# Relative bias of the neighbourhood heads: added by VectorE to mirrored scores instead of by flip products on TensorE

## The chip, the cores and the metric

One core of one Trainium2 chip runs the whole program. The metric is the device time of one launch in microseconds, median over runs. The kernel before takes 879.6 us (three runs, 878.18 to 881.19).

## The reference

Two layers (DEPTH = 2) of a pre-norm encoder on one sequence of 256 tokens (a grid of 4 rows by 64 columns), width 1024, all float32:

```python
for l in range(DEPTH):
    h = rms_norm(x, norm1_g[l])
    aq, ak, av, bq, bk, bv, cq, ck, cv, c_q, c_kv, k_rope = split(h @ w_in[l])
    o_a = global attention (RMS-normed, axially rotated q and k), 4 heads
    o_b = neighbourhood_attention(bq, bk, bv, b_rel_bias[l]), 4 heads
    o_c = windowed attention with a distance penalty and a sink, 4 heads
    o_d = latent attention (low-rank q and kv, shared rotary key), 4 heads
    y = einsum(stack(o_a, o_b, o_c, o_d), w_branch[l])
    g = sigmoid(h @ w_gate[l] + b_gate[l])
    x = x + sum_n(g * y) @ w_o[l]
    h2 = rms_norm(x, norm2_g[l])
    x = x + square(relu(h2 @ w_ff1[l])) @ w_ff2[l]
return rms_norm(x, final_g)
```

In the neighbourhood attention a query at grid row r and column c sees all 4 rows (the window of 8 is cut to the grid's 4) and 16 columns clamped to the grid. To the scaled score with the key at row kr, column kc it adds `rel_bias[head, kr - r + 7, kc - c + 15]`, from a table of 15 x 31 for each head. Every other key is out.

## The kernel before

**Numbers.** Each float32 product with weights is made of three products of a high and a low part (`split_product`, L1035 to L1037). ScalarE rounds a chunk of weights to its high part (`split_hi`, w_hi, L537), VectorE subtracts for the low part (`split_lo`, w_lo, L734). The weights come in chunks of 1 MB (w_in: 1.05 MB, 8 chunks of 268 columns), each in two halves, by SP's queue into `raw`, which holds two chunks. A half is loaded again as soon as VectorE has made the low part of what it held. w_hi and w_lo are rings of four chunks, so TensorE can be up to three chunks behind the splits.

**Stages.** The mixer part of a layer is a list of steps that all engines walk in program order: steps 0 to 7 are the eight chunks of w_in (`project`, tokens on the partitions: first half for token tile 0, second for tile 1; ScalarE copies the first out at L671, VectorE the second at L959), then 16 gate chunks and the four branch products `y`. In a step each engine also does a piece of the attention. The heads go in pairs: the pair j has its scores on TensorE (`scores`) in step 8 + 2j, its softmax on VectorE and ScalarE (`maxima`, `exps`, `normalise`) a step later, its transposes of the probabilities (`turn_prob`) in step 10 + 2j, its values a step after that. Pairs 0 and 1 are of mixer A, 2 and 3 of B (the neighbourhood heads, n = 1), 4 and 5 of C, 6 and 7 of D. Small transposes and products (`small`) go through one bank, bank_x; ScalarE empties it (`evac`), and the next of them waits for that. On ScalarE the order in step 6 is: `evac` of aq (the transposed queries of mixer A), copy of the projection's first half, `split_hi` of chunk 9. In step 5 it is: copy, `split_hi` of chunk 8, the first gate chunk.

**The bias.** POOL issues 16 DMAs in each layer (L493, after `rs_a`, that is in step 3), one for each head, token tile and grid row of queries, each from 64 overlapping runs of the table into 64 partitions: 4 key rows of 64 elements (256 bytes) for each partition. The partition axis counts the queries backwards, so that the address in the table rises with the partition. When all 16 are in, POOL adds the column mask `window` (L498). TensorE then starts the scores of the B pairs with a product of `flip` (the reversed identity times 8, the inverse of the scale) with the bias (L1118), which turns the rows round and adds them, and accumulates the scores on top (L1126). A score product runs on two 64-row halves of TensorE, a flip product on all 128 rows. The buffer `bias` is used again for `qd` and `kd`, the latent mixer's queries and keys, which ScalarE writes from step 15 on (uq0, L584).

**What sets the order.** The order on each engine is the order of the code. VectorE and ScalarE wait for semaphores only, and an instruction that waits holds up all behind it on its engine. POOL's `norm` and `inverse_root` (L453) make the reciprocal roots that the norms need.

Of the kernel before, what the change touches and what calls it, by code (L numbers as in the profile page):

```python
# [34 lines left out]
BIAS_ROW = 2 * NA_COLS - 1  # L35
WINDOW = 128
# [91 lines left out]
C_FLIP = C_WIN + GRID_W  # L128
C_N = C_FLIP + P

# [5 lines left out]
DVE_LINKS, POOL_LINKS = 50, 12  # L136


def constants():
# [19 lines left out]
    def tiles(a):  # L159
        return a.reshape(T, P, -1).transpose(1, 0, 2).reshape(P, -1)  # L160

    parts = [np.eye(P, dtype=np.float32), tiles(np.concatenate([rc, cc], 1)), tiles(np.concatenate([rs, cs], 1)),
             tiles(dc), tiles(ds), tiles(dist), window, np.eye(P, dtype=np.float32)[::-1] * HD ** 0.5]
# [5 lines left out]
def trunk_kernel(nc, x, norm1_g, w_in, w_gate, b_gate, a_q_norm_g, a_k_norm_g, b_rel_bias, c_sink,  # L169
# [3 lines left out]
    with ctx:  # L173
# [21 lines left out]
        bias = sb("bias", [P, H, T * SEQ])  # L195
        bias_flat = bias[:, :, :].rearrange("p a b -> p (a b)")
# [12 lines left out]
        tmp = sb("tmp", [P, 2, 512])  # L209
        vd = sb("vd", [P, T, H, HD])  # L210
# [36 lines left out]
        flip = cst[:, C_FLIP:C_FLIP + P]  # L247
# [72 lines left out]
        stored = sem("stored")  # L320

        def f32(ap):
            return ap.bitcast(F32)
# [100 lines left out]
        def _(pool):  # L424
# [40 lines left out]
            with pool.Fori(0, DEPTH) as l:  # L465
                norm(2 * l, l)

                pool.dma_start(gain_qk[:, 0, :], a_q_norm_g[bass.ds(l, 1), :].to_broadcast([P, HD])).then_inc(gains_landed, 16)
# [13 lines left out]

                for hd in range(H):
                    for t in range(T):
                        for r in range(2):
                            row = 2 * t + 1 - r
                            at = (NA_ROWS - 1 - row) * BIAS_ROW + NA_COLS - 1 - (GRID_W - 1)
                            table_h = b_rel_bias[bass.ds(l, 1), hd]
                            src = bass.AP(tensor=table_h.tensor, offset=table_h.offset + at,
                                          ap=[[1, GRID_W], [BIAS_ROW, ROWS], [1, GRID_W]])  # L490
                            dst = bias[r * GRID_W:(r + 1) * GRID_W, hd, t * SEQ:(t + 1) * SEQ].rearrange(
                                "p (r c) -> p r c", c=GRID_W)
# [12 lines left out]
                for k in range(4 * (NB - 1)):  # L505
                    pool.wait_ge(y_read, l * 16 + (k + 5))
                    if k >= 4:
                        pool.wait_ge(mixed, l * 12 + (k - 3))
                    nc.gpsimd.tensor_tensor(mix[:, k % 4, :], mix[:, k % 4, :], tmp[:, k % 2, :], ALU.add).then_inc(mixed, 1)  # L509
                norm(2 * l + 1, l)  # L510
# [9 lines left out]
        def _(act):  # L520
# [42 lines left out]
            def evac(step, l):  # L563
# [6 lines left out]
                if name in ("aq", "bq", "cq"):  # L570
# [49 lines left out]
            def heads_hi(i, l):  # L620
# [5 lines left out]
                if n >= 2:  # L626
                    act.wait_ge(w_used, used_count(l, POS["y", n - 2]))
                nc.scalar.activation(part_hi[:, n % 2, blk, :], bank_o[:, blk * SEQ:(blk + 1) * SEQ],
                                     ACT.Copy).then_inc(o_hi_ready, 1)
# [74 lines left out]
        def _(dve):  # L704
# [154 lines left out]
            def maxima(i, l):  # L859
# [5 lines left out]
                scale = (DQ if n == 3 else HD) ** -0.5  # L865
                if n == 2:
# [24 lines left out]
            def heads_lo(i, l):  # L891
                n, _, blk, half = HEADS[i]
                if half == 0:
                    return
                dve.wait_ge(o_hi_ready, l * (NH // 2) + (i // 2 + 1))
                nc.vector.tensor_tensor(part_lo[:, n % 2, blk, :], bank_o[:, blk * SEQ:(blk + 1) * SEQ],
                                        f32(part_hi[:, n % 2, blk, :]), ALU.subtract).then_inc(o_lo_ready, 1)
# [115 lines left out]
        def _(pe):  # L1013
# [91 lines left out]
            def scores(j, l):  # L1105
# [6 lines left out]
                if n == 1:  # L1112
                    pe.wait_ge(bias_ready, l + 1)
                for t in range(T):
                    keys = slice(t * SEQ, (t + 1) * SEQ)
                    if n == 1:
                        for half in range(2):
                            nc.tensor.matmul(bank_acc[:, half, keys], flip, bias[:, HEADS[2 * j + half][1], keys],  # L1118
                                             start=True, stop=False)
                    for half in range(2):  # L1120
# [5 lines left out]
                        ins = nc.tensor.matmul(bank_acc[:, half, keys], q[:, t * P:(t + 1) * P], k, start=(n != 1), stop=True)  # L1126
# [198 lines left out]
```

## Time and profile before

| | |
|---|---|
| median of 3 runs | 879.6 us (878.18 to 881.19) |
| the profiled execution, its own time | 882.37 us |
| its span (first to last instruction) | 880.7 us |
| TensorE busy, matmuls | 841.5 us, 96% |
| VectorE / ScalarE / POOL busy | 509.9 / 428.3 / 100.1 us |
| mean granted TensorE clock | 0.985 |
| moved by DMA | 142.49 MB, mean 162 GB/s |

A row of the timeline gives start, busy time, engine, line, operation, output and inputs, the count of instructions merged in it and, in brackets, how long the engine stood idle before it and what ended the idle time. Matmuls are pipelined, so their durations overlap: what one costs is the distance of starts, not the duration. A float32 matmul stands in the trace as two records. TensorE's granted clock is given as a share of full speed: 1.00 is 2.4 GHz and 0.50 is 1.2 GHz.

### The profile page before, as it was taken

The page shows a single profiled execution, that of the slowest core. Times are in us where ns is not written, and L with a number is a line of the kernel's source. Part 1 is how long each engine was busy: PE and PEld are TensorE (multiplying, and loading weights), DVE is VectorE, ACT ScalarE, POOL GpSimd, SP SyncE. Part 2 cuts the span into 40 slices and gives each one's busy share as a digit, 9 for nine tenths or more (in the row PEclk, how much of TensorE's full clock was granted, in tenths as well). Part 3 has the DMA queues.
Part 4 walks back from the last instruction along what each step waited for, and adds up shares of the span by engine and source line. Part 5 has one row for each costly group of instructions (what it writes and reads, how often), then busy time and mean ns, then how long its engine had stood idle before and what let it go on. Part 6 is the DMA issues. An engine that isn't in the chain of part 4 may idle for free.

```text
span 880.7 us, 16075 instructions
## 1 busy us (share of the span) xinstructions
PE 841.5 (96%) x5861; PEld 770.1 (87%) x5861; DVE 509.9 (58%) x712; ACT 428.3 (49%) x712; POOL 100.1 (11%) x129
## 2 busy tenths in 40 slices
PE   6977999999999999999989699999999999999996
PEld 6977987999979999999889698889998899999995
DVE  4647644777555555555457474468566655555553
ACT  6315744755454444444364265555643644444441
POOL 4432000112200000000025200002112100000000
PEclk9997999999999999999999899999999999999999
DMA  8886543354346555555459575234453565555541
GB/s 257 228 144 202 141 144 105 105 149 135 120 150 213 190 188 183 180 181 187 138 147 205 137 224 145 96 120 123 142 190 103 168 221 185 181 183 187 181 145 49
DMA packets 101630, 142.49 MB, mean 162 GB/s; under 512 B 5244, under 2 KB 87424, under 8 KB 101568
## 3 DMA queue, kind: packets, MB, share of 16 engines
q1 hardware_dynamic: 99296, 137.12, 48.7%
q0 software_dynamic: 1984, 4.43, 4.1%
q8 instruction: 38, 0.62, 0.3%
q14 instruction: 24, 0.20, 0.1%
q10 hardware_dynamic: 288, 0.11, 0.0%
HBM read 140.60 MB, written 1.05 MB: 161 GB/s over the span
## 4 chain that ended last, share of the span: by engine, by line
issue 67%; PE 21%; POOL 7%; DMA 3%; POOLq 1%; DVE 0%; DVEq 0%; ACT 0%; ACTq 0%
PE bank_w L1035 4%; PE bank_w L1037 4%; PE bank_w L1036 3%; DMA bias<-in_b_rel_bias 3%; PE bank_acc L1035 3%; PE bank_acc L1036 3%; PE bank_acc L1037 3%; POOL mix L509 2%; POOL bias L498 1%; POOL bias L493 1%; POOL nsink L476 1%; POOL rstd L463 0%; POOL mean L462 0%; POOL ss_a L452 0%; POOL rs_d L453 0%
## 5 line engine op out<-in xcount | busy, mean ns | idle before, releaser
L734 DVE TENSOR_TENSOR w_lo<-raw,w_hi 128x1024 fp32r<-128x1024 f32 (+1 forms) x256 | 314.1, 1277 | 72.5 <-ACT w_hi L537 72.2
L1035 PE MATMUL bank_w<-act_hi,w_hi 128*128 128x256 f32 x1024 | 292.9, 286 | 2.5 <-DVE act_lo L746 2.2
L1037 PE MATMUL bank_w<-act_hi,w_lo 128*128 128x256 f32 x1024 | 290.3, 283 | 0.0
L1036 PE MATMUL bank_w<-act_lo,w_hi 128*128 128x256 f32 x1024 | 289.8, 283 | 0.0
L537 ACT ACTIVATE w_hi<-raw 128x1024 fp32r<-128x1024 f32 (+1 forms) x256 | 257.0, 1060 | 63.5 <-DMA raw<-in_w_gate 35.2
L1035 PEld LDWEIGHTS bank_w<-act_hi,w_hi 128*128 128x128 f32 x1024 | 194.6, 190 | 9.8 <-issue 6.1
L1036 PEld LDWEIGHTS bank_w<-act_lo,w_hi 128*128 128x128 f32 x1024 | 193.9, 189 | 1.7 <-issue 0.5
L1037 PEld LDWEIGHTS bank_w<-act_hi,w_lo 128*128 128x128 f32 x1024 | 194.2, 190 | 0.0
L646 ACT ACTIVATE big<-bank_w 128x512 f32<-128x512 f32 x32 | 19.2, 599 | 185.5 <-PE bank_w L1037 185.5
L932 DVE TENSOR_TENSOR big<-big 128x512 f32<-128x512 f32 x32 | 22.2, 693 | 147.5 <-ACT big L646 147.5
L1036 PE MATMUL bank_acc<-w_lo,part_hi 128*128 128x512 f32 x256 | 100.3, 392 | 0.0
L1035 PE MATMUL bank_acc<-w_hi,part_hi 128*128 128x512 f32 x256 | 100.2, 391 | 0.0
L1037 PE MATMUL bank_acc<-w_hi,part_lo 128*128 128x512 f32 x256 | 99.8, 390 | 0.0
L1035 PE MATMUL bank_w<-w_hi,act_hi 128*128 128x268 f32 x256 | 75.7, 296 | 0.5 <-DVE act_lo L746 0.4
L1036 PE MATMUL bank_w<-w_lo,act_hi 128*128 128x268 f32 x256 | 74.7, 292 | 0.0
L1037 PE MATMUL bank_w<-w_hi,act_lo 128*128 128x268 f32 x256 | 74.6, 291 | 0.0
L638 ACT ACTIVATE big<-bank_w,vec 128x256 f32<-128x256 f32 x64 | 26.9, 471 | 82.5 <-PE bank_w L1037 82.5
L509 POOL TENSOR_TENSOR mix<-mix,tmp 128x512 f32<-128x512 f32 x24 | 35.4, 1490 | 262.5 <-DVE tmp L923 262.0
L1037 PEld LDWEIGHTS bank_acc<-w_hi,part_lo 128*128 128x128 f32 x256 | 48.1, 188 | 10.6
L1035 PEld LDWEIGHTS bank_acc<-w_hi,part_hi 128*128 128x128 f32 x256 | 48.1, 188 | 9.5
L1036 PEld LDWEIGHTS bank_acc<-w_lo,part_hi 128*128 128x128 f32 x256 | 48.0, 188 | 8.9
L1035 PEld LDWEIGHTS bank_w<-w_hi,act_hi 128*128 128x128 f32 x256 | 49.8, 195 | 0.9 <-DVE act_lo L746 0.9
(156 smaller groups left out, 1000.1 us busy)
## 6 DMA issues: line engine op xcount, KB each, us to landing
raw<-in_w_ff SPq DMA_DIRECT2D x128, 512.0 KB, 4.8
raw<-in_w_gate SPq DMA_DIRECT2D x64, 512.0 KB, 5.0
raw<-in_w_in SPq DMA_DIRECT2D x32, 536.0 KB, 5.9
raw<-in_w_o SPq DMA_DIRECT2D x16, 512.0 KB, 4.3
raw<-in_w_branch SPq DMA_DIRECT2D x16, 256.0 KB, 4.2
raw<-in_w_branch SPq DMA_DIRECT2D x8, 512.0 KB, 4.4
bias<-in_b_rel_bias POOLq DMA_DIRECT2D x32, 64.0 KB, 8.0
xs<-in_x SPq DMA_DIRECT2D x2, 512.0 KB, 4.1
```

Source lines behind the costliest of these rows:

```text
L476: nc.gpsimd.tensor_tensor(nsink[:, :], sink[:, :], neg_one[:, :], ALU.mult).then_inc(nsink_ready, 1)
L493: pool.dma_start(dst, src).then_inc(bias_landed, 16)
L498: nc.gpsimd.tensor_tensor(rows, rows, window.unsqueeze(1).to_broadcast([P, H * T * ROWS, GRID_W]), ALU.add).then_inc(bias_ready, 1)
L509: nc.gpsimd.tensor_tensor(mix[:, k % 4, :], mix[:, k % 4, :], tmp[:, k % 2, :], ALU.add).then_inc(mixed, 1)
L537: nc.scalar.activation(half_view(w_hi, c, h), raw_half(c, h), ACT.Copy).then_inc(w_hi_ready, 1)
L638: ins = nc.scalar.activation(big[:, i % 8, d * SEQ:(d + 1) * SEQ], bank[:, d * SEQ:(d + 1) * SEQ], ACT.Tanh, bias=vec[:, BG + 2 * i + d:BG ...
L646: nc.scalar.activation(relu[b], bank_w[:, b, :], ACT.Relu).then_inc(relu_ready, 1)
L734: nc.vector.tensor_tensor(half_view(w_lo, c, h), raw_half(c, h), f32(half_view(w_hi, c, h)), ALU.subtract).then_inc(w_lo_ready, 1)
L932: nc.vector.tensor_tensor(sq[b], relu[b], relu[b], ALU.mult).then_inc(u_squared, 1)
L1035: nc.tensor.matmul(dst, s_hi, m_hi, start=first, stop=False)
L1036: nc.tensor.matmul(dst, s_hi, m_lo, start=False, stop=False)
L1037: ins = nc.tensor.matmul(dst, s_lo, m_hi, start=False, stop=last)
```

## The change

The bias of one head is now loaded as one run for each partition: two DMAs in a layer (one for each parity of the grid row), each of 64 partitions x 4 heads x 219 elements (876 bytes). They land in `run`, a view of `tmp`, and are issued by POOL right after the first `norm`, ahead of its other small loads. A run of 219 elements holds six overlapping blocks of 64 that start 31 apart (SLOTS = 6); token tile 0 uses blocks 2 to 5 and tile 1 blocks 0 to 3. POOL copies the six blocks of a head into `bias` and adds the mask in the same instruction, four instructions of 128 x 384 in place of one of 128 x 2048, right after `rs_a`.

The flip products are gone, and `flip` with them. Instead ScalarE writes the transposed queries of mixer B with each tile of 128 reversed (`mirrored`, at bq), so the scores come out with their rows in the order of the bias, and VectorE adds the bias to them in PSUM, one instruction for each token tile, before the row maxima. The outputs of the heads come out mirrored too, and are turned back where ScalarE and VectorE read them (`heads_hi`, `heads_lo`). ScalarE's write of `qd` in the old place of the bias now waits until VectorE has used the bias of the last B head (uq0 waits for top_ready). POOL waits for its own last sum before the second norm.

The core of the diff:

```diff
+                for r in range(2):
+                    at = (NA_ROWS - 4 + r) * BIAS_ROW + NA_COLS - GRID_W
+                    tables = b_rel_bias[bass.ds(l, 1), 0]
+                    src = bass.AP(tensor=tables.tensor, offset=tables.offset + at,
+                                  ap=[[1, GRID_W], [(2 * NA_ROWS - 1) * BIAS_ROW, H], [1, RUN]])
+                    pool.dma_start(run[r * GRID_W:(r + 1) * GRID_W, :, :], src).then_inc(bias_landed, 16)
                 pool.dma_start(gain_qk[:, 0, :], ...
...
+                pool.wait_ge(cst_landed, 16)
+                pool.wait_ge(bias_landed, l * 32 + 32)
                 for hd in range(H):
-                    for t in range(T):
-                        for r in range(2):
...
-                            src = bass.AP(tensor=table_h.tensor, offset=table_h.offset + at,
-                                          ap=[[1, GRID_W], [BIAS_ROW, ROWS], [1, GRID_W]])
...
-                            pool.dma_start(dst, src).then_inc(bias_landed, 16)
-
-                pool.wait_ge(cst_landed, 16)
-                pool.wait_ge(bias_landed, l * (16 * H * T * 2) + 16 * H * T * 2)
-                rows = bias_flat.rearrange("p (r c) -> p r c", c=GRID_W)
-                nc.gpsimd.tensor_tensor(rows, rows, window.unsqueeze(1).to_broadcast([P, H * T * ROWS, GRID_W]),
-                                        ALU.add).then_inc(bias_ready, 1)
+                    blocks = bass.AP(tensor=run.tensor, offset=run[:, hd, :].offset,
+                                     ap=[run.ap[0], [BIAS_ROW, SLOTS], [1, GRID_W]])
+                    ins = nc.gpsimd.tensor_tensor(bias[:, hd, :, :], blocks,
+                                                  window.unsqueeze(1).to_broadcast([P, SLOTS, GRID_W]), ALU.add)
+                ins.then_inc(bias_ready, 1)
...
+        def mirrored(ap):
+            return bass.AP(tensor=ap.tensor, offset=ap.offset + P - 1,
+                           ap=[*ap.ap[:-1], [P, ap.shape[-1] // P], [-1, P]])
...
+                if name == "bq":
+                    ins = nc.scalar.activation(qT[1].rearrange("p b (t s) -> p b t s", t=T), mirrored(x2), ACT.Copy)
...
                 elif name in ("uq0", "uq1"):
                     t = int(name[-1])
+                    if t == 0:
+                        act.wait_ge(top_ready, l * NH + 2 * H)
...
+                if n == 1:
+                    dve.wait_ge(bias_ready, l + 1)
+                    for t in range(T):
+                        st = s[:, t * SEQ:(t + 1) * SEQ]
+                        seen = bias[:, hd, 2 - 2 * t:2 - 2 * t + ROWS, :].rearrange("p r c -> p (r c)")
+                        ins = nc.vector.scalar_tensor_tensor(out=st, in0=seen, scalar=1.0 / scale, in1=st,
+                                                             op0=ALU.mult, op1=ALU.add)
+                    chained(ins, l)
...
-                if n == 1:
-                    pe.wait_ge(bias_ready, l + 1)
                 for t in range(T):
                     keys = slice(t * SEQ, (t + 1) * SEQ)
-                    if n == 1:
-                        for half in range(2):
-                            nc.tensor.matmul(bank_acc[:, half, keys], flip, bias[:, HEADS[2 * j + half][1], keys],
-                                             start=True, stop=False)
```

On TensorE, in step 12 of a layer (the scores of the first B pair), the kernel before has this in a row (bank_x is the small bank, cst holds the identity and `flip`):

```order
L1085 MATMUL bank_x<-cst,qkv 128x128 x2
L1118 MATMUL bank_acc<-bias,cst 128x256 x2
L1126 MATMUL bank_acc<-qk_ab 128x256 x2
L1118 MATMUL bank_acc<-bias,cst 128x256 x2
L1126 MATMUL bank_acc<-qk_ab 128x256 x2
L1138 MATMUL bank_acc<-cst,prob 128x128 x8
```

and the changed kernel this, with the last gate product ahead of it and the first one behind:

```order
L1058 MATMUL bank_w<-act_hi,w_hi 128x256
L1080 REGISTER_ALU
L1106 MATMUL bank_x<-cst,qkv 128x128 x2
L1141 MATMUL bank_acc<-qk_ab 128x256 x4
L1153 MATMUL bank_acc<-cst,prob 128x128 x8
L1210 REGISTER_ALU
L1056 MATMUL bank_w<-act_hi,w_hi 128x256
```

The four flip products of the pair are gone, and nothing has come in their place.

On POOL, from the first norm of a layer to the sums of the mixers, the kernel before has (ISA and REGISTER_ALU rows in between left out; 16 of the L493 DMAs, one shown):

```order
L463 TENSOR_TENSOR rstd<-mean,neg_half 128x1
...
L468 DMA gain_qk<-in_a_q_norm_g 128x64
L469 DMA gain_qk<-in_a_k_norm_g 128x64
...
L470 DMA sink<-in_c_sink 128x4
...
L476 TENSOR_TENSOR nsink<-sink,neg_one 128x4
...
L453 TENSOR_TENSOR rs_a<-ss_a,neg_half 128x12
...
L493 DMA bias<-in_b_rel_bias 64x4x64
...
L498 TENSOR_TENSOR bias<-bias,cst 128x2048
```

and the changed kernel:

```order
L469 TENSOR_TENSOR rstd<-mean,neg_half 128x1
...
L479 DMA tmp<-in_b_rel_bias 64x4x219
...
L480 DMA gain_qk<-in_a_q_norm_g 128x64
L481 DMA gain_qk<-in_a_k_norm_g 128x64
...
L482 DMA sink<-in_c_sink 128x4
...
L488 TENSOR_TENSOR nsink<-sink,neg_one 128x4
...
L459 TENSOR_TENSOR rs_a<-ss_a,neg_half 128x12
...
L500 TENSOR_TENSOR bias<-tmp,cst 128x384 x4
```

The bias loads have moved ahead of all of POOL's other loads, and the work that followed them now stands directly behind `rs_a`.

On VectorE, at the softmax of a B pair (step 13), the changed kernel has, for one of the two heads and the split behind them:

```order
L881 SCALAR_TENSOR_TENSOR bank_acc<-bias,bank_acc 128x256 x2
L721 REGISTER_ALU
L888 TENSOR_REDUCE top<-bank_acc 128x2
L721 REGISTER_ALU
L895 TENSOR_SCALAR ntop<-top 128x2
L743 REGISTER_ALU
L744 TENSOR_TENSOR w_lo<-raw,w_hi 128x1024
```

The first row, two additions of the bias, is new; what stands behind it is as before.

## Rows read from the trace of the kernel before

**Rows 1.** The page's engines: busy us (share of the span) and count.
```profile
PE 841.5 (96%) x5861; PEld 770.1 (87%) x5861; DVE 509.9 (58%) x712; ACT 428.3 (49%) x712; POOL 100.1 (11%) x129
```

**Rows 2.** TensorE's waits: us in total, times, longest.
```profile
PE bank_x L1085 <- ACT qk_ab L571: 17.8, 2, 10.3
```

**Rows 3.** Timeline of ScalarE, layer 0, steps 5 and 6.
```profile
51.21 0.40 ACT L671 ACTIVATE qkv<-bank_w 128x268 f32<-128x268 f32 x1 [1.26 <-PE bank_w L1037]
67.75 1.06 ACT L537 ACTIVATE w_hi<-raw 128x1024 fp32r<-128x1024 f32 x1 [16.15 <-DMA raw<-in_w_gate]
...
70.18 0.58 ACT L571 ACTIVATE qk_ab<-bank_x 128x512 f32<-128x512 f32 x1
```

**Rows 4.** DMA queues and issues, 41.8 to 67.7 us; last row: gate loads, whole run.
```profile
q0 software_dynamic: 512, 1.05, 54.7%
q1 hardware_dynamic: 2585, 2.60, 31.6%
...
raw<-in_w_gate SPq DMA_DIRECT2D x4, 512.0 KB, 19.3
bias<-in_b_rel_bias POOLq DMA_DIRECT2D x16, 64.0 KB, 8.3
...
raw<-in_w_gate SPq DMA_DIRECT2D x64, 512.0 KB, 5.0
```

**Rows 5.** Windows of 10 us: busy (count) by engine, PEclk, DMA share, GB/s.
```profile
70.80:80.80 10.00, 9.98 (x66) 9.99 (x67) 7.30 (x8) 5.39 (x8) 0.91 (x1) 0.78 0.61 201
80.80:90.80 10.00, 10.00 (x84) 9.46 (x83) 7.30 (x14) 6.41 (x15) 1.43 (x3) 1.00 0.68 223
501.30:511.30 10.00, 9.70 (x66) 9.70 (x67) 7.91 (x7) 5.03 (x8) 1.51 (x1) 0.80 0.58 189
```

**Rows 6.** Timeline of TensorE, scores of a B pair and of a C pair.
```profile
114.42 1.03 PE L1118 MATMUL bank_acc<-bias,cst 128*128 128x256 f32 x4
...
117.70 1.09 PE L1138 MATMUL bank_acc<-cst,prob 128*128 128x128 f32 x8
...
153.15 1.13 PE L1126 MATMUL bank_acc<-qk_c 64*128 64x256 f32 x8
154.21 1.10 PE L1138 MATMUL bank_acc<-cst,prob 128*128 128x128 f32 x8
```

**Rows 7.** Timeline of VectorE and ScalarE at the softmax of B and C pairs.
```profile
117.80 0.69 DVE L870 TENSOR_REDUCE top<-bank_acc 128x2 f32<-128x512 f32 x1 [5.58 <-PE bank_acc L1126]
...
134.68 0.69 DVE L870 TENSOR_REDUCE top<-bank_acc 128x2 f32<-128x512 f32 x1 [5.38 <-PE bank_acc L1126]
...
154.31 0.69 DVE L868 SCALAR_TENSOR_TENSOR bank_acc<-cst,bank_acc 128x512 f32<-128x512 f32 x1 [3.66 <-PE bank_acc L1126]
...
137.20 0.49 ACT L584 ACTIVATE bias<-bank_x 128x384 f32<-128x384 f32 x1 [0.84 <-PE bank_x L1093]
```

**Rows 8.** Timeline of POOL, VectorE and TensorE around the mask's addition and mixer A's norm.
```profile
39.15 2.30 POOL L453 TENSOR_TENSOR rs_a<-ss_a,neg_half 128x12 f32<-128x12 f32 x1
...
67.19 4.51 POOL L498 TENSOR_TENSOR bias<-bias,cst 128x2048 f32<-128x2048 f32 x1 [15.96 <-DMA bias<-in_b_rel_bias]
...
50.85 0.96 DVE L808 TENSOR_TENSOR qkv<-mix 128x768 f32<-128x768 f32 x1
...
68.84 5.08 DVE L734 TENSOR_TENSOR w_lo<-raw,w_hi 128x1024 fp32r<-128x1024 f32 x2 [14.22 <-ACT w_hi L537]
...
53.98 0.60 PE L1081 MATMUL bank_x<-cst,qkv 128*128 128x128 f32 x4
```

**Rows 9.** Timeline of ScalarE: copies of the first two projections, layers 0 and 1.
```profile
21.59 0.43 ACT L671 ACTIVATE qkv<-bank_w 128x268 f32<-128x268 f32 x1
27.48 0.40 ACT L671 ACTIVATE qkv<-bank_w 128x268 f32<-128x268 f32 x1 [5.45 <-PE bank_w L1037]
...
456.43 0.37 ACT L671 ACTIVATE qkv<-bank_w 128x268 f32<-128x268 f32 x1
461.06 0.40 ACT L671 ACTIVATE qkv<-bank_w 128x268 f32<-128x268 f32 x1 [4.26 <-PE bank_w L1037]
```

More of the change, by code:

```diff
@@ L35 @@
 BIAS_ROW = 2 * NA_COLS - 1
+SLOTS = ROWS + 2
+RUN = (SLOTS - 1) * BIAS_ROW + GRID_W
 WINDOW = 128
@@ L127 @@
 C_WIN = C_DIST + T * SEQ
-C_FLIP = C_WIN + GRID_W
-C_N = C_FLIP + P
+C_N = C_WIN + GRID_W
 WARM = (4, 3, 2)
-DVE_LINKS, POOL_LINKS = 50, 12
+DVE_LINKS, POOL_LINKS = 54, 12
 def constants():
@@ L162, in constants @@
     parts = [np.eye(P, dtype=np.float32), tiles(np.concatenate([rc, cc], 1)), tiles(np.concatenate([rs, cs], 1)),
-             tiles(dc), tiles(ds), tiles(dist), window, np.eye(P, dtype=np.float32)[::-1] * HD ** 0.5]
+             tiles(dc), tiles(ds), tiles(dist), window]
     table = np.ascontiguousarray(np.concatenate(parts, 1), dtype=np.float32)
@@ L194, in trunk_kernel @@
         sq = [big[:, 6 + b, :] for b in range(2)]
-        bias = sb("bias", [P, H, T * SEQ])
-        bias_flat = bias[:, :, :].rearrange("p a b -> p (a b)")
+        bias = sb("bias", [P, H, SLOTS, GRID_W])
+        bias_flat = bias[:, :, :, :].rearrange("p h s c -> p (h s c)")
         qd = bias_flat[:, 0:T * H * DQ].rearrange("p (t h d) -> p t h d", t=T, h=H)
@@ L209, in trunk_kernel @@
         tmp = sb("tmp", [P, 2, 512])
+        run = tmp[:, :, :].rearrange("p a b -> p (a b)")[:, 0:H * RUN].rearrange("p (h x) -> p h x", h=H)
         vd = sb("vd", [P, T, H, HD])
@@ L246, in trunk_kernel @@
         dist = cst[:, C_DIST:C_DIST + T * SEQ]
-        flip = cst[:, C_FLIP:C_FLIP + P]
         window = cst[:, C_WIN:C_WIN + GRID_W]
@@ L509, in _ @@
                     nc.gpsimd.tensor_tensor(mix[:, k % 4, :], mix[:, k % 4, :], tmp[:, k % 2, :], ALU.add).then_inc(mixed, 1)
+                pool.wait_ge(mixed, l * 12 + 12)
                 norm(2 * l + 1, l)
@@ L627, in heads_hi @@
                     act.wait_ge(w_used, used_count(l, POS["y", n - 2]))
-                nc.scalar.activation(part_hi[:, n % 2, blk, :], bank_o[:, blk * SEQ:(blk + 1) * SEQ],
-                                     ACT.Copy).then_inc(o_hi_ready, 1)
+                dst, src = part_hi[:, n % 2, blk, :], bank_o[:, blk * SEQ:(blk + 1) * SEQ]
+                if n == 1:
+                    dst, src = dst.rearrange("p (t s) -> p t s", t=T), mirrored(src)
+                nc.scalar.activation(dst, src, ACT.Copy).then_inc(o_hi_ready, 1)
             def gate(i, l):
@@ L895, in heads_lo @@
                 dve.wait_ge(o_hi_ready, l * (NH // 2) + (i // 2 + 1))
-                nc.vector.tensor_tensor(part_lo[:, n % 2, blk, :], bank_o[:, blk * SEQ:(blk + 1) * SEQ],
-                                        f32(part_hi[:, n % 2, blk, :]), ALU.subtract).then_inc(o_lo_ready, 1)
+                dst, src = part_lo[:, n % 2, blk, :], bank_o[:, blk * SEQ:(blk + 1) * SEQ]
+                hi = f32(part_hi[:, n % 2, blk, :])
+                if n == 1:
+                    dst, src, hi = dst.rearrange("p (t s) -> p t s", t=T), mirrored(src), hi.rearrange("p (t s) -> p t s", t=T)
+                nc.vector.tensor_tensor(dst, src, hi, ALU.subtract).then_inc(o_lo_ready, 1)
             def mix_lo(q, l):
@@ L1125, in scores @@
                             q, k = qT[n][rows, blk, :], kT[n][rows, blk if n == 1 else 0, :]
-                        ins = nc.tensor.matmul(bank_acc[:, half, keys], q[:, t * P:(t + 1) * P], k, start=(n != 1), stop=True)
+                        ins = nc.tensor.matmul(bank_acc[:, half, keys], q[:, t * P:(t + 1) * P], k, start=True, stop=True)
                         if t == T - 1:
```

8 lines of the change are left out of this document (2 added, 6 removed).

## The prediction

> **What bounds the kernel now.** I read the page's engine shares first: TensorE is busy 96% of the span, the others 58% at most [rows 1]. So a microsecond off TensorE's own list is a microsecond off the end, and the others count only where TensorE waits. Then its list of waits: one stands out, 17.8 us in two waits, 10.3 and so 7.5, one in each layer, before the transposes of ak [rows 2]. These need the small bank, which ScalarE empties of aq. The timeline of ScalarE says why it is late: it copies the projection at 51.21, then stands 16.15 us before the high part of the first gate chunk, and takes aq only at 70.18 [rows 3]. The releaser named is the load of that chunk. The view of the DMA queues over that stretch says what the load met: the gate loads took 19.3 us to land there and 5.0 in the median of the run, while the queue of POOL's loads, which are the 16 bias loads alone, took 54.7% of all 16 engines' time for 1.05 MB and the weights 31.6% for 2.60 MB [rows 4]. Of 25.9 us that is 14.2 us of all engines for the bias and 8.2 for the weights: per MB 13.5 against 3.2. The bias moves in 16 x 64 x 4 = 4096 runs of 256 bytes.
>
> Last, the windows behind the two waits: TensorE is busy all the time in them but at a granted clock of 0.78 and 0.80, partly the lower level of 1.2 GHz, after it stood idle; the window of equal length after the first has 1.00 [rows 5].
>
> **The change part by part.** *Flip products.* In a B pair the scores start at 114.42 and the transposes behind them at 117.70, 3.28 us; in a C pair, which has the same eight score records and no flips, 153.15 to 154.21, 1.06 us [rows 6]. The changed order on TensorE is that of the C pair. 2.22 us x 2 pairs x 2 layers = 8.9 us off TensorE.
>
> *Bias loads.* 32 loads of 64 KB become 4, in each layer 2 x 64 x 4 = 512 runs of 876 bytes, 0.45 MB, issued at the layer's start. Step 3 has none left. Without them the gate load should take about its usual 5.0 us, some 14 us less than 19.3 [rows 4]. ScalarE's 16.15 us then shrink to about 2, and aq is out at 70.18 - 14.3 = 55.9; TensorE asks for the bank 10.3 us before it gets it, about 60.5. That is a margin of over 4 us, so I count both waits as gone: 17.8 us. What is late next in step 6 is nothing by this reckoning. The clock comes back with it: 66 records in the first 10 us against 84, 18 x 0.12 = 2.1 us; in layer 1 66 records in 9.70 busy us where 81.5 would fit, 1.8 us [rows 5]. Together 3.9 us.
>
> What the new loads cost is not in the trace. At the weights' price per MB they take 1.4 us of all engines, at the old runs' price per byte 6.1, at their price per run (512 of 4096) 1.8. I take 1.8, since 876-byte runs are near to the weights' rows. They meet the load of chunk 2, whose split stands ahead of ScalarE's copy of the first projection. A projection takes 27.48 - 21.59 = 5.9 us, and its first bank is wanted again half of that after the copy could start; the copy takes 0.43, so layer 0 has 2.95 - 0.43 = 2.5 us of room. In layer 1 the copies stand 4.63 apart, so the first was 1.3 late, and 1.2 are left [rows 9]. 1.8 us fit into the one and exceed the other by 0.6 if all of it falls on that load: I take 0.5 us. The ends are 0 and (6.1 - 2.5) + (6.1 - 1.2) = 8.5.
>
> The Trainium skill (DMA: Bandwidth & Descriptors, section Specifications) gives 512 bytes as the least transfer for line rate. The trace sides with it as far as 256-byte runs go, at 13.5 us per MB against 3.2 [rows 4]; no row has a run of 876 bytes that does not start on a round address.
>
> *POOL's addition of the mask.* It was one instruction of 4.51 us at 67.19. Now it is four of 384 columns, 4.51 x 384 / 2048 = 0.85 each, 3.4 us, directly behind rs_a, that is from 41.45 [rows 8], in VectorE's chain that makes mixer A's queries. That chain ends at 51.81 and TensorE takes its result at 53.98, so it has 2.2 us. How the two engines disturb each other the old place shows: VectorE's two subtractions took 5.08 us from 68.84, and ended 2.2 us after POOL's end at 71.70 [rows 8], so the first did not get on before POOL was through. If all 3.4 us were added, 1.2 would be lost in each layer; if the four instructions slip into VectorE's gaps, none. I take 0.5 each, 1.0 us.
>
> *VectorE's additions.* Two instructions of 128 x 256 for each head; the like one of C takes 0.69 us for 512 columns [rows 7], so 0.7 us a head and 1.4 a pair, 5.6 us in the run. VectorE stands idle 5.58 and 5.38 us before the maxima of the two B pairs [rows 7], waiting for TensorE, and the probabilities are wanted only in the step after. I cost them at nothing. If that cover were gone it would be 5.6 us.
>
> *The wait of uq0.* ScalarE takes uq0 at 137.20. The maxima of the pair start at 134.68 and were done 1.7 us later [rows 7]; with 1.4 more they end at 137.8. So ScalarE waits some 0.6 us. Queued behind it are the exponentials of that pair, which need the same maxima, and a weight split three chunks ahead. The next user of the small bank on TensorE comes behind a whole branch product. Nothing.
>
> *Mirrored reads.* ScalarE and VectorE read PSUM backwards in five instructions of a layer. No row shows one. Between no extra cost and a doubling of 0.5 us each it is at most 2.5 us in a layer, on engines that wait for TensorE; I take zero. The new wait in front of the second norm is for POOL's own work, long done. Gains, sink and latent weights land some microseconds later; the first of them is used in step 3.
>
> *Sum.* Against the profiled execution's own 882.4 us: 882.4 - 8.9 - 17.8 - 3.9 + 0.5 + 1.0 = 853.3. That execution lies 2.8 us over the median of 879.6, so 850.5 us is forecast.
>
> **The rivals.** *Early collision (0.12).* The bias loads cost 6.1 us a layer, by the byte price of the old ones, and hold up chunk 2. Then TensorE waits 3.6 and 4.9 us near the start of each layer, and may lose some clock again, up to the 3.9 us of above: 850.5 + 8 + up to 3.9, about 861. For it: the other weights of POOL's queue land in the same microseconds. Against it: 876 bytes are long runs, and in layer 1 the loads start while few weights move.
>
> *VectorE held up by POOL (0.10).* All 3.4 us fall on the chain of aq: 1.2 + 1.2 in place of 1.0, so 852. For it: the 5.08 us [rows 8]. Against it: four short instructions with ends between them. The Trainium skill (SBUF — State Buffer, section SBUF: two separate sides) has a port pair that is locked for a whole instruction, by a VectorE instruction with two SBUF inputs or a GpSimd one that reads SBUF, and by that rule every overlap here is a full block; the 5.08 us agree.
>
> *The wait stays (0.06).* The gate load was late not by the bias loads but by the way SP's queue and the two raw buffers meet at the change from w_in to gates. Then only the flips are won: 879.6 - 8.9 + 1.5 = 872. Against it: the same kind of load lands in 5.0 us elsewhere, and POOL's queue held more than half of the engines' time [rows 4].
>
> *The runs fall apart (0.04).* This is the case that ends slower. If the overlapping source were moved element by element, a layer's bias would be 2 x 64 x 4 x 219 = 112,128 pieces. At the old price of a run, 14.2 us / 4096 = 3.5 ns of all engines, that is 390 us a layer, of which nearly all is a wait of the B pairs and the weights: far above 1200 us. It decides from about 17 us of engine time a layer, some 4900 pieces, where it eats the gain. Against it: the old source has the same unit step, and was moved in 256-byte runs.
>
> **How the numbers follow.** The forecast has 0.68, alone with 847 to 855. With no new cost it is 879.6 - 30.6 = 849.0; some other DMA waits of ScalarE may shrink too, so the low end is 846. The high end of 860 takes in the second rival and most of the first. A difference under 0.3% can't be told from none here. All cases but the last are faster by more: 0.95; within 0.3% 0.01, slower 0.04.
>
> **What would show it.** TensorE's wait for ScalarE before the ak transposes gone or under 1 us; gate loads of step 5 landing in 5 to 7 us; the scores of a B pair 1.1 us long; TensorE's clock at 1.00 through steps 6 and 7; POOL's queue under 3 us of all engines at a layer's start; VectorE idle about 4 us before the maxima of a B pair. I am wrong if a new wait of TensorE appears in steps 0 to 2, or before aq in step 6, or if ScalarE still stands for the first gate chunk by more than 9 us.

## The result, and the profile after

The changed kernel takes 853.74 us (median of four runs, 853.13 to 854.21) against 879.67 of the kernel before beside it (four runs, 878.18 to 881.19): ratio 0.9701, 95% interval 0.968 to 0.9722. Its profiled execution took 854.21 us with a span of 852.5, at a mean granted clock of 0.994. The forecast was 850.5 us, with a range of 846 to 860. Between the profiled executions the gain is 882.37 - 854.21 = 28.2 us (29.1 forecast), between the medians 25.9.

The page's engine row answers to [rows 1]: TensorE has 32 records fewer, VectorE 16 more, and POOL is busy 20 us less.

```profile
PE 827.8 (97%) x5829; PEld 760.7 (89%) x5829; DVE 513.8 (60%) x728; ACT 428.1 (50%) x712; POOL 79.7 (9%) x107
```

TensorE's waits (total, times, longest) answer to [rows 2]. No wait for aq's evacuation is left; the last row here is new.

```profile
PE bank_o L1069 <- DVE big L750: 6.0, 5, 3.3
PE bank_w L1042 <- DMA cst<-in_table: 4.8, 1, 4.8
PE bank_w L1056 <- DVE act_lo L756: 2.6, 3, 1.1
PE bank_acc L1069 <- ACT big L556: 2.2, 1, 2.2
PE bank_w L1056 <- ACT qkv L681: 1.7, 1, 1.7
```

ScalarE in steps 5 and 6, against [rows 3]: the first gate chunk comes 0.99 us after ScalarE is free for it, not 16.15, and aq is out at 56.44, not 70.18. (L541 is the old L537, L577 the old L571.)

```profile
51.62 0.40 ACT L681 ACTIVATE qkv<-bank_w 128x268 f32<-128x268 f32 x1 [3.55 <-PE bank_w L1058]
53.01 1.06 ACT L541 ACTIVATE w_hi<-raw 128x1024 fp32r<-128x1024 f32 x1 [0.99 <-DMA raw<-in_w_gate]
55.48 1.07 ACT L541 ACTIVATE w_hi<-raw 128x1024 fp32r<-128x1024 f32 x1 [1.41 <-DMA raw<-in_w_gate]
56.44 0.58 ACT L577 ACTIVATE qk_ab<-bank_x 128x512 f32<-128x512 f32 x1
```

Windows of steps 6 and 7 in both layers, against [rows 5]: 83 records each at a granted clock of 1.00, the level of 2.4 GHz throughout, where the windows behind the old waits had 66 at 0.78 and 0.80.

```profile
56.00:66.00 10.00, 10.00 (x83) 10.00 (x83) 5.39 (x6) 5.64 (x9) 0.00 (x0) 1.00 0.86 267
66.00:76.00 10.00, 10.00 (x83) 9.46 (x83) 8.15 (x13) 4.52 (x8) 1.42 (x3) 1.00 0.71 224
475.00:485.00 10.00, 10.00 (x83) 10.00 (x83) 5.04 (x6) 5.29 (x8) 0.00 (x0) 1.00 0.88 271
```

The scores of the first B pair on TensorE take 103.47 - 102.41 = 1.06 us, as those of C in [rows 6]:

```profile
102.41 1.13 PE L1141 MATMUL bank_acc<-qk_ab 64*128 64x256 f32 x8
103.47 0.77 PE L1153 MATMUL bank_acc<-cst,prob 128*128 128x128 f32 x5
```

VectorE at the same pair, against [rows 7]: it still stands idle 3.46 us before the new additions, each pair of which takes 0.76.

```profile
103.57 0.76 DVE L881 SCALAR_TENSOR_TENSOR bank_acc<-bias,bank_acc 128x256 f32<-128x256 f32 x2 [3.46 <-PE bank_acc L1141]
104.37 0.69 DVE L888 TENSOR_REDUCE top<-bank_acc 128x2 f32<-128x512 f32 x1
105.09 0.17 DVE L895 TENSOR_SCALAR ntop<-top 128x2 f32<-128x2 f32 x1
105.26 0.76 DVE L881 SCALAR_TENSOR_TENSOR bank_acc<-bias,bank_acc 128x256 f32<-128x256 f32 x2
```

POOL's additions beside VectorE's norm of mixer A, in the order of the two engines, against [rows 8]:

```profile
39.57 2.30 POOL L459 TENSOR_TENSOR rs_a<-ss_a,neg_half 128x12 f32<-128x12 f32 x1
41.85 3.74 POOL L500 TENSOR_TENSOR bias<-tmp,cst 128x384 f32<-128x384 f32 x4
...
43.10 3.25 DVE L791 TENSOR_TENSOR mix<-qkv,rs_a 128x128 f32<-128x128 f32 x6
...
52.65 0.96 DVE L818 TENSOR_TENSOR qkv<-mix 128x768 f32<-128x768 f32 x1
```

Before, the same six products of VectorE took 1.29 us, from 42.68:

```profile
42.68 1.29 DVE L781 TENSOR_TENSOR mix<-qkv,rs_a 128x128 f32<-128x128 f32 x6
```

They were 2.0 us longer, where 2.5 us of them lay beside POOL's additions, and ended at 46.35, soon after POOL's end at 45.59. The Trainium skill (SBUF — State Buffer, section SBUF: two separate sides) has an exclusive lock between a VectorE instruction with two SBUF inputs and a GpSimd one that reads SBUF, held for a whole instruction. That most of the overlap was lost agrees. Yet the chain's last result came at 53.6 and TensorE took it at 54.39, without a wait.

The new wait stands at the start of layer 1. TensorE's row, and ScalarE's around it (against [rows 9]):

```profile
443.38 0.39 PE L1056 MATMUL bank_w<-w_hi,act_hi 128*128 128x268 f32 x1 [1.67 <-ACT qkv L681]
```

```profile
439.53 1.10 ACT L541 ACTIVATE w_hi<-raw 128x1072 fp32r<-128x1072 f32 x1 [2.54 <-DMA raw<-in_w_in]
441.95 1.10 ACT L541 ACTIVATE w_hi<-raw 128x1072 fp32r<-128x1072 f32 x1 [1.32 <-DMA raw<-in_w_in]
442.95 0.38 ACT L681 ACTIVATE qkv<-bank_w 128x268 f32<-128x268 f32 x1
446.65 0.40 ACT L681 ACTIVATE qkv<-bank_w 128x268 f32<-128x268 f32 x1 [3.32 <-PE bank_w L1058]
```

The queues there (428 to 440 us) say why: POOL's queue, now with the bias in front, holds the DMA engines half the time, and the w_in halves take 7.5 us to land.

```profile
q0 software_dynamic: 445, 1.07, 49.5%
q1 hardware_dynamic: 991, 1.03, 27.6%
...
raw<-in_w_in SPq DMA_DIRECT2D x3, 536.0 KB, 7.5
tmp<-in_b_rel_bias POOLq DMA_DIRECT2D x2, 219.0 KB, 4.0
```

In the same stretch of the kernel before (445 to 457 us) the w_in halves took 5.4 us, and POOL's queue had this:

```profile
q0 software_dynamic: 288, 0.63, 30.1%
```

So of the 5.9 us of all engines that POOL's queue takes here, 3.6 were its other loads, there before, and 2.3 are the bias.

**An account by landmarks**, the same instruction in both traces:

```
                                      before    after     step
first copy of layer 0 (ScalarE)        21.59     21.98    +0.4
scores of the first B pair (PE)        114.42    102.41   -12.4   wait 10.3, clock 2.1
norm at the end of layer 0            437.50    421.11    -4.4   two pairs of flips
second copy of layer 1                461.06    446.65    +2.0   new wait of 1.67 in it
end of the span                       880.7     852.5    -13.8   wait and clock 9.3, flips 4.4
```

The gains are 30.6 us, where 30.6 were forecast, the losses 2.4. The 0.4 us of layer 0 can't be put down to the change: the same kernel in experiment 11 has its first copy at 21.45, and version 5, with no bias load this early, at 23.19. The step in layer 1 repeats. From the norm at the end of layer 0 to the second copy of layer 1 it takes 25.2 to 25.5 us in the four profiled executions with long loads at the layer's start (the changed kernel twice, experiments 1 and 9), and 23.4 to 24.6 in all others but experiment 3.

### The profile page after: what moved, and what is told of

The parts are those of the page before. It is cut to its first block, busy times and chain, and to the rows that moved or that the text cites. A ratio compares the mean times of both kernels' runs of the same rounds, so it can differ in the third digit from the quotient of the medians.

```text
span 852.5 us, 15967 instructions
## 1 busy us (share of the span) xinstructions
PE 827.8 (97%) x5829; PEld 760.7 (89%) x5829; DVE 513.8 (60%) x728; ACT 428.1 (50%) x712; POOL 79.7 (9%) x107
## 3 DMA queue, kind: packets, MB, share of 16 engines
HBM read 139.33 MB, written 1.05 MB: 165 GB/s over the span
## 4 chain that ended last, share of the span: by engine, by line
PE 94%; DMA 2%; DVE 1%; issue 1%; ACT 0%; POOL 0%; SPq 0%; DVEq 0%; POOLq 0%; ACTq 0%
PE bank_w L1056 20%; PE bank_w L1058 20%; PE bank_w L1057 20%; PE bank_acc L1056 9%; PE bank_acc L1057 9%; PE bank_acc L1058 9%; PE bank_acc L1141 2%; DMA raw<-in_w_in 2%; PE bank_o L1170 2%; PE bank_acc L1153 2%; DVE w_lo L744 1%; PE bank_x L1118 0%; PE bank_x L1123 0%; PE bank_x L1102 0%; PE bank_x L1114 0%
## 5 line engine op out<-in xcount | busy, mean ns | idle before, releaser
L744 DVE TENSOR_TENSOR w_lo<-raw,w_hi 128x1024 fp32r<-128x1024 f32 (+1 forms) x256 | 308.2, 1254 | 43.1 <-ACT w_hi L541 42.8
L541 ACT ACTIVATE w_hi<-raw 128x1024 fp32r<-128x1024 f32 (+1 forms) x256 | 256.1, 1058 | 34.2 <-DMA raw<-in_w_in 17.5
```

The source lines that it names most:

```text
L541: nc.scalar.activation(half_view(w_hi, c, h), raw_half(c, h), ACT.Copy).then_inc(w_hi_ready, 1)
L744: nc.vector.tensor_tensor(half_view(w_lo, c, h), raw_half(c, h), f32(half_view(w_hi, c, h)), ALU.subtract).then_inc(w_lo_ready, 1)
```

## The experiments

All comparisons are medians in device microseconds; each group of runs had the kernel before beside it (880.21 us for experiments 1 to 4, 880.12 for 5, 8, 9 and 10, 879.42 for 6, 7, 11 and 12). A difference of about 1 us between variants of different groups is not told from none.

**1. The new loads alone, flip products kept.** The additions and mirrored reads of the change are left out, the flips read the new layout.

```diff
+  pool.dma_start(run[r * GRID_W:(r + 1) * GRID_W, :, :], src).then_inc(bias_landed, 16)
...
-  pool.dma_start(dst, src).then_inc(bias_landed, 16)
...
-  nc.tensor.matmul(bank_acc[:, half, keys], flip, bias[:, HEADS[2 * j + half][1], keys],
+  nc.tensor.matmul(bank_acc[:, half, keys], flip, bias[:, HEADS[2 * j + half][1], 2 - 2 * t:2 - 2 * t + ROWS, :].rearrange("p r c -> p (r c)"),
```

> The new loads (two DMAs of 876-byte runs at the layer's start, four mask additions) with the old flip products on TensorE and nothing mirrored. Theory (two separate gains): the wait for aq in step 6 is gone in both layers, the flips stay, so it lies 8.9 us above the changed kernel, 862.6 us; TensorE's waits before ak zero, its wait for the first copy in layer 1 again 1.5 to 2 us. Rival (the flips were hidden and the loads are the whole gain): 854 us, as the changed kernel.

Measured: 863.92 us (862.48 to 864.63), ratio 0.9813 (0.9786 to 0.9841). No wait for aq is left, and the early wait is there too:

```profile
PE bank_w L1042 <- ACT qkv L677: 1.2, 1, 1.2
```

So the loads bring 16.3 us, and the rest of the change about 10.

**2. The mirrored scores alone, old loads.** The flips are out, VectorE adds; the 16 loads and POOL's one addition stay.

```diff
+  ins = nc.scalar.activation(qT[1].rearrange("p b (t s) -> p b t s", t=T), mirrored(x2), ACT.Copy)
...
+  seen = bias[:, hd, t * SEQ:(t + 1) * SEQ]
+  ins = nc.vector.scalar_tensor_tensor(out=st, in0=seen, scalar=1.0 / scale, in1=st,
...
-  nc.tensor.matmul(bank_acc[:, half, keys], flip, bias[:, HEADS[2 * j + half][1], keys],
```

> Mirrored queries and VectorE's additions, no flips, but the old 16 loads of 256-byte runs behind rs_a. Theory: the B pairs lose 2.2 us of scores four times and the wait in step 6 stays whole at 10 and 7.5 us: 879.7 - 8.9 = 870.8 us. Rival 1 (the additions on VectorE lie on TensorE's path): up to 5.6 us more, 876. Rival 2 (the wait in step 6 came with the flips): near 854.

Measured: 871.03 us (869.48 to 873.52), ratio 0.9902 (0.9874 to 0.993). The gain is 9.2 us, by the forecast's 8.9 for the flips. The wait stays, in this execution at 13.0 us (17.8 were expected), and POOL's queue, with the same loads in the same 25.9 us, takes 12.3 us of all engines where it took 14.2:

```profile
PE bank_x L1109 <- ACT qk_ab L580: 13.0, 2, 6.6
q0 software_dynamic: 512, 1.05, 47.3%
```

The two halves add up: 16.3 + 9.2 = 25.5.

**3. The old short loads, but at the layer's start** (nothing else changed).

```diff
+  pool.dma_start(dst, src).then_inc(bias_landed, 16)      # the loops over hd, t, r, ahead of gain_qk
...
-  pool.dma_start(dst, src).then_inc(bias_landed, 16)      # behind rs_a
```

> The kernel before with its 16 short-run DMAs only moved to the layer's start, flips kept. Theory (the number of short runs is what costs, wherever they stand): 14.2 us of all 16 engines now meet chunks 2 to 4 of w_in, the wait moves from step 6 to steps 0 to 2 and is 10 us or more in each layer: 875 to 890 us, step 6 without a wait. Rival (the place was the cost, since at the layer's start the ring of weights is not yet needed): as with the long runs there, 862 us.

Measured: 890.13 us (888.75 to 891.09), ratio 1.011 (1.0082 to 1.0138): slower than before. The old wait is gone and a larger one has come at the start of each layer:

```profile
PE bank_w L1035 <- ACT qkv L671: 23.3, 2, 13.7
```

In 14 to 40 us the queues read so, and the five w_in halves issued there took 18.0 us to land:

```profile
q0 software_dynamic: 800, 1.67, 59.7%
...
raw<-in_w_in SPq DMA_DIRECT2D x5, 536.0 KB, 18.0
```

Moving the loads off step 3 is not what brings the gain.

**4. The new loads in the old place.** The changed kernel with its two loads behind `rs_a`.

```diff
-  pool.dma_start(run[r * GRID_W:(r + 1) * GRID_W, :, :], src).then_inc(bias_landed, 16)   # ahead of gain_qk
...
+  pool.dma_start(run[r * GRID_W:(r + 1) * GRID_W, :, :], src).then_inc(bias_landed, 16)   # behind rs_a
```

> The changed kernel with its two long-run DMAs moved back to the old place behind rs_a. Theory (short runs cost, not the place): the loads take about 1.8 us of all engines there, the first gate chunk lands at most 2 us later than now, no wait in step 6, and the 1.7 us wait at the start of layer 1 shrinks to nothing: 852 us. Rival (the place): a wait of 7 to 10 us in step 6 of each layer comes back, about 870 us.

Measured: 853.94 us (852.8 to 855.6), ratio 0.9705 (0.9677 to 0.9732), level with the changed kernel; the 852 expected were not reached. The bias meets the gate loads as before, and delays them no more; 41.8 to 67.7 us, against [rows 4]:

```profile
q0 software_dynamic: 160, 0.45, 7.2%
...
raw<-in_w_gate SPq DMA_DIRECT2D x8, 512.0 KB, 5.0
tmp<-in_b_rel_bias POOLq DMA_DIRECT2D x2, 219.0 KB, 5.5
```

7.2% of 25.9 us are 1.87 us of all engines, beside the forecast's 1.8. The form of the loads decides, not their place. TensorE has no wait at the start of layer 1 here, but 0.7 us in two before aq: POOL's additions now start at 48.01, beside later products of the same chain on VectorE, which take 3.61 us and not 1.15.

```profile
48.62 3.61 DVE L811 TENSOR_TENSOR mix<-mix,cst 128x192 f32<-128x192 f32 x4
```

**5. The new loads in pieces.** Version 4 with each load cut into six by columns: 12 loads, 3072 runs of 148 bytes (136 in the last piece), 0.45 MB as there.

```diff
+  for a in range(0, RUN, 37):
+      n = min(37, RUN - a)
+      src = bass.AP(tensor=tables.tensor, offset=tables.offset + at + a,
+                    ap=[[1, GRID_W], [(2 * NA_ROWS - 1) * BIAS_ROW, H], [1, n]])
```

> The loads in the old place behind rs_a, the same 0.45 MB a layer, but in 12 DMAs of at most 37 elements (148 bytes), 3072 runs in place of 512. Theory (price per run, 3.5 ns of all engines): 10.6 us of all engines a layer, the first gate chunk some 9 us later than with long runs there, a wait of TensorE before ak of 3 to 5 us in each layer: 861 to 866 us. Rival (price per byte): 1.9 us of all engines, no wait, 854 us.

Measured: 852.89 us (852.36 to 853.64), ratio 0.9686 (0.9669 to 0.9703), and no wait before aq. In the same stretch:

```profile
q0 software_dynamic: 384, 0.45, 11.5%
```

That is 3.0 us of all engines, 0.97 ns a run, where the old loads took 14.2 / 4096 = 3.5 ns. The price for each short run, on which I had built, fell here: shorter runs were cheaper than the old ones.

**6. The kernel before with its loads grouped another way.** The same 4096 runs of 256 bytes and 1.05 MB in 16 loads behind `rs_a`, the flips kept. A load takes one key row over four heads, where it took four rows of one head.

```diff
-  for hd in range(H):
+  for k in range(ROWS):
...
-                    ap=[[1, GRID_W], [BIAS_ROW, ROWS], [1, GRID_W]])
+                    ap=[[1, GRID_W], [(2 * NA_ROWS - 1) * BIAS_ROW, H], [1, GRID_W]])
...
+      c = t * SEQ + k * GRID_W
+      pool.dma_start(bias[r * GRID_W:(r + 1) * GRID_W, :, c:c + GRID_W], src).then_inc(bias_landed, 16)
```

> The kernel before with its flip products kept, its 16 loads in the old place behind the running sums, and the same 4096 runs of 256 bytes (1.05 MB) in a layer. Only the grouping differs: each load now takes one row of the key tile over four heads, where it took four neighbouring rows of one head, whose 256 runs all read within some 880 bytes of memory. If the cost lies in many runs that read the same few hundred bytes at the same time, queue 0 falls from 54.7% of the 25.9 us (14.2 us of all engines) to 4 to 6 us, the wait in step 6 falls to 0 to 2 us and the time to about 864 us (863 to 868), as with the new loads and the flips. If each short run costs the same wherever it reads, queue 0 stays at 13 to 15 us and the time at 880 us (877 to 883).

Measured: 861.16 us (860.38 to 862.85), ratio 0.9793 (0.9775 to 0.981), with no wait for aq. Its queues in 41.8 to 67.7 us:

```profile
q1 hardware_dynamic: 4902, 4.92, 63.9%
q0 software_dynamic: 512, 1.05, 24.6%
...
raw<-in_w_gate SPq DMA_DIRECT2D x8, 512.0 KB, 5.5
bias<-in_b_rel_bias POOLq DMA_DIRECT2D x16, 64.0 KB, 4.2
```

The same runs and bytes, in as many loads and packets (512), cost 24.6% of 25.9 = 6.4 us of all engines (4 to 6 expected), not 14.2, and the weights moved 4.92 MB instead of 2.60. So neither the number of runs nor their length made the old loads dear, but which runs stand together in a load. And 18.3 us of the change's gain can be had by this regrouping alone, with no other edit; the new loads alone gave 16.3 (experiment 1). The time came out 2 us below the 863 to 868 that were expected. These loads don't stand at the layer's start: from the norm to the second copy in layer 1 it takes 23.6 us here and 25.2 in experiment 1, which can be most of the 2 us. The regrouping together with the mirrored scores was not run.

**7. The long runs, one load for each head.** Version 4 with 8 loads (one head and parity each, 512 runs of 876 bytes).

```diff
-  pool.dma_start(run[r * GRID_W:(r + 1) * GRID_W, :, :], src)             # x2
+  pool.dma_start(run[r * GRID_W:(r + 1) * GRID_W, hd:hd + 1, :], src)     # x8
```

> The kernel with the long loads late, its runs of 876 bytes regrouped from 2 loads over four heads to 8 loads, one for each head and parity (512 runs, 0.45 MB as before). If runs that read the same stretch of memory at the same time are what costs, queue 0 takes 3 to 4 us of all engines in 41.8 to 67.7 us where it took 1.87; the wait before the key transposes does not come back, and the time is 853 to 855 us. If the place read is of no account, queue 0 takes 1.8 to 2.0 us and the time is 853.9 us (853 to 855). Only the queue's time tells the two apart; over 857 us would speak against both.

Measured: 853.48 us (852.53 to 853.68), ratio 0.97 (0.9685 to 0.9716). The queue's row:

```profile
q0 software_dynamic: 256, 0.45, 7.7%
```

2.0 us against 1.87. My theory that runs which read one small stretch of memory are dear asked for 3 to 4, and fell in this form: here every load reads within (63 + 219) x 4 = 1128 bytes and pays nothing for it. Version 6 changed two things at once: what the runs of a load read, and how they lie in SBUF (four pieces apart, where they were 1 KB in one piece). Which of them, or the 256 runs a load against 64 here, makes the price is open. TensorE waits 1.2 us in two before aq here, as in experiment 4.

**8. No bias loads at all** (the bias is left out; POOL adds the mask to zeros).

```diff
+  nc.gpsimd.memset(run[:, :, :], 0.0)     # once
-  pool.dma_start(run[r * GRID_W:(r + 1) * GRID_W, :, :], src).then_inc(bias_landed, 16)
```

> The changed kernel without any load of the bias: the runs are zeros, so the bias is left out of the result; the additions and the rest of the work stay. Theory: it takes off what the early loads still cost, the 2.4 us by which layer 1 and layer 0 start later than before: 851.3 us. Rival (that lateness has another cause, such as the longer list of loads on POOL): 853.7 us.

Measured: 852.7 us (852.01 to 853.63), ratio 0.9684 (0.9667 to 0.9702), no wait at the start of layer 1. The early loads cost the changed kernel about 1.0 to 1.3 us by the medians (853.74 and 854.02 against 852.7), near what this measurement can tell; the theory had 851.3, the rival 853.7. The traces agree: from the norm to the second copy in layer 1 it takes 24.55 us here and 25.54 in the changed kernel.

**9. VectorE's additions doubled**, each made twice with half the bias.

```diff
-  ins = nc.vector.scalar_tensor_tensor(out=st, in0=seen, scalar=1.0 / scale, in1=st,
+  ins = nc.vector.scalar_tensor_tensor(out=st, in0=seen, scalar=0.5 / scale, in1=st,    # in two loops over the tiles
```

> The changed kernel with each addition of the bias on VectorE made twice at half the factor, 16 instructions more in the run, 6.4 us of VectorE's time. Theory (VectorE's idle time covers it): 853.7 us, VectorE idle some 2 us before the additions. Rival (the additions already lie on TensorE's path): 857 to 860 us.

Measured: 855.97 us (854.78 to 856.44), ratio 0.9716 (0.9698 to 0.9734): 2.2 us over the changed kernel by the medians, between the 853.7 of the theory and the 857 of the rival (against the runs of before beside each, the difference is 1.3 to 1.8). But the trace lies 1.23 us behind already where the first addition starts (104.80 against 103.57), after a wait of 1.91 us in step 0 that the change did not touch:

```profile
18.36 0.39 PE L1062 MATMUL bank_w<-w_hi,act_hi 128*128 128x268 f32 x1 [1.91 <-DVE act_lo L756]
104.80 0.76 DVE L881 SCALAR_TENSOR_TENSOR bank_acc<-bias,bank_acc 128x256 f32<-128x256 f32 x2 [3.46 <-PE bank_acc L1147]
105.60 0.76 DVE L887 SCALAR_TENSOR_TENSOR bank_acc<-bias,bank_acc 128x256 f32<-128x256 f32 x2
```

Nearly all of this stands already at the first copy (23.19 against 21.98), and version 5, which has no doubled additions, has its first copy at 23.19 too: it is not their doing. From the first addition to the layer's end (the norm, 422.75 against 421.11) the trace loses 0.41 us more, and from the second copy of layer 1 to the end of the span 0.37. So doubled additions cost some 0.4 us in a layer where their own time is 3.2, and single ones are covered to within that. With the 1.2 us this makes the trace's 2.0; why the first steps took longer is not shown.

**10. Loads and additions spread.** The changed kernel with the loads behind `nsink`, after POOL's other loads, and the additions behind VectorE's end of mixer A's norm.

```diff
-  pool.dma_start(run[r * GRID_W:(r + 1) * GRID_W, :, :], src).then_inc(bias_landed, 16)   # ahead of gain_qk
...
   nc.gpsimd.tensor_tensor(nsink[:, :], sink[:, :], neg_one[:, :], ALU.mult).then_inc(nsink_ready, 1)
+  pool.dma_start(run[r * GRID_W:(r + 1) * GRID_W, :, :], src).then_inc(bias_landed, 16)
...
+  pool.wait_ge(a_ready, l + 1)
   pool.wait_ge(bias_landed, l * 32 + 32)
```

> The changed kernel with its two bias loads issued behind the negated sink (about 26 us into layer 0) and POOL's four additions of the mask behind the end of mixer A's norm on VectorE. Theory: the early collision (1.7 us wait and 0.4 us more in layer 1, 0.4 us in layer 0) goes and nothing takes its place, the six multiplications of the norm take 1.3 us again and not 3.25: 851.5 us. Rival (the loads cost the same wherever they stand while w_in is loaded): 853.7 us.

Measured: 852.17 us (852.0 to 853.1), ratio 0.9682 (0.9665 to 0.97), for 851.5 expected. TensorE has no wait for ScalarE's copy and none before aq, and VectorE's six products take 1.29 us again. At the start of layer 1 (428 to 440 us) POOL's queue holds nearly the same share as in the changed kernel, but the w_in halves land in 5.5 us, not 7.5:

```profile
q0 software_dynamic: 436, 1.07, 46.6%
```

The total is the same; the bias now comes behind the other loads. So the share of a stretch alone does not say what a queue delays: it matters which loads it meets.

**11 and 12. The changed kernel and version 10 once more, on one chip.**

> The changed kernel as it is, to be compared on one chip with the version whose loads and additions are spread. Expected 853.7 us (853 to 855).

> The changed kernel with its bias loads behind the last norm input and POOL's additions behind the normalized halves, once more beside the changed kernel. If the early collision (2.4 us in the landmarks) is what it takes away, it comes out 1.5 to 2 us below the changed kernel on the same chip: 852.2 us (851.5 to 853). The rival, that the difference seen before was one of chips, gives the same time for both, within 0.5 us.

Measured: 854.02 us (853.62 to 855.49), ratio 0.9716 (0.97 to 0.9733), and 853.21 (851.98 to 854.32), ratio 0.9703 (0.9685 to 0.9721). The wait at layer 1's start is 1.5 us in the one, 0.6 in the other:

```profile
PE bank_w L1056 <- ACT qkv L681: 1.5, 1, 1.5
```

```profile
PE bank_w L1057 <- ACT qkv L682: 0.6, 1, 0.6
```

Version 10 is 0.8 us below the change here and was 1.6 below it before, so the 1.5 to 2 expected were not reached, and the intervals overlap. It has the lowest median of all (852.17), but is not shown to be faster.

## Why the prediction was right

*Flip products, 8.9 us.* Right: 2.2 us a pair in the landmarks (4.4 a layer), 9.2 us alone in experiment 2.

*The two waits, 17.8 us, and the clock, 3.9.* Right in cause and size. With regrouped loads alone (experiment 6) the profiled executions differ by 882.37 - 861.16 = 21.2 us, for 21.7 forecast. The rival in which SP's queue and the raw buffers made the wait, and it stayed, is out by experiments 1, 4 and 6. aq was out at 56.44 (55.9 forecast).

*The price of the new loads.* The 1.8 us of all engines was right (1.87 in experiment 4), its reason was not. I took the old loads' price for each run; experiments 5 and 6 show prices of 0.97 and 1.6 ns of all engines for short runs that had cost 3.5. The rule of 512 bytes (the Trainium skill, DMA: Bandwidth & Descriptors, section Specifications), with which I let the trace side at 256 bytes, does by them not account for most of the old loads' price: runs of 148 and 256 bytes, in loads over four heads, left the gate loads at 4.7 and 5.5 us. Short runs do stay dearer by the byte, 6.6 and 6.1 us of all engines for each MB against 4.2 at 876 bytes, on the side of that rule; the old loads' 13.5 are twice that.

*The early collision, 0.5 us.* The mis-sized term: 2.0 us in layer 1 by the landmarks, 1.0 to 1.3 by experiment 8; the 0.4 us of layer 0 are within what executions differ by. Two signs that the prediction had set for itself came out against it here. It called itself wrong if a new wait of TensorE appeared in steps 0 to 2, and one of 1.67 us did. It asked for POOL's queue under 3 us of all engines at a layer's start, and it took 5.9: the 3.6 of POOL's other loads had not been counted, and the bias took 2.3, not 1.8. I had set 1.8 us against 1.2 us of room as if the bias met w_in alone; but POOL's other loads stand behind it in the same queue, and ScalarE stood 2.54 and 1.32 us for w_in. So the rival of an early collision came true in kind, at a quarter or less of its 8.5 us.

*POOL's additions, 1.0 us.* They took 3.74 us (3.4 forecast) and cost nothing in the changed kernel, though VectorE was held up by 2.0 us, more than half of the 3.4 I had as the upper end: the chain's result was ready at 53.6 and TensorE asked at 54.4. With later loads the margin is gone and TensorE waits 0.7 us in two (experiment 4).

*VectorE's additions at nothing.* Right to within some 0.4 us a layer (experiment 9). The wait of uq0 for them was 1.8 us in each layer, not 0.6, and cost nothing, as argued.

*The runs fall apart, and the slower case.* Did not come: 219 elements moved as runs.

*From the profiled execution to the median, -2.8 us.* Most of the miss. In medians the result lies 853.7 - 850.5 = 3.2 us over the forecast: 0.9 stood already between the profiled executions (854.2 for 853.3: losses of 2.4 for 1.5), and 2.3 us come from this step: the profiled execution of before lay 2.8 us over its median, that of after only 0.5 over its own. The runs of before spread from 876.6 to 884.5 us (11 runs of the first group), those of the versions without the wait by 1 to 3; but in the other groups the kernel before spreads by 3.0 to 3.9 only. So the surplus of that execution probably lay in the wait itself, which the same sum removed, and should not have been taken off twice. That the wait varies between executions is seen in experiment 2 (13.0 us for 17.8); that the surplus lay there is argued, not shown.

## What to carry to other kernels

A wait that names a weight load can be another queue's doing: look at what share of the DMA engines each queue holds in that stretch and how long the loads take to land there. Try the other queue's loads in another grouping before a larger change: here that alone gave 18.3 us, where the whole change gave 25.9. When work moves into a new place, count everything that is already queued there, not the new piece alone. A stall that one profiled execution shows is a sample; if the change removes it, its excess over the usual goes with it and must not be subtracted again.

## What the runs showed of the hardware

- 4096 runs of 256 bytes cost 14.2 us of all 16 DMA engines (12.3 in experiment 2) as four rows of one head in a load, 6.4 us as four heads in a load; 3072 runs of 148 bytes 3.0 us; 512 runs of 876 bytes 1.87 us in 2 loads and 2.0 in 8.
- While POOL's queue held 54.7% of the engines, SP's loads of 512 KB took 19.3 us to land; at 59.7% those of 536 KB 18.0; at 7.2% those of 512 KB 5.0. At the start of layer 1, 49.5% went with 7.5 us for 536 KB, and 46.6% with 5.5 where the bias stood last in POOL's queue (experiment 10).
- Six products of VectorE took 3.25 us with POOL's additions beside them and 1.29 alone. POOL's four additions took 7.46 us where they met VectorE's splits (experiment 10), 3.74 in the changed kernel.
- Mirrored reads of PSUM cost nothing that these runs can tell: experiment 2 gained 9.2 us with them, 8.9 being the flips.
